# Second mixer: decay chain and gate rows in PSUM, weight splits between the activations, gate products at the third tile

## The reference

```
z = a_lr @ w_alpha_up + b_alpha
log_a = log_sigmoid(z) / 16                       # 4 heads x 128 channels
G = cumsum(log_a) within a chunk
q_dec = q * 128**-0.5 * exp(G); k_inv = k * exp(-G)
A = causal(q_dec @ k_inv.T); o = A @ v + (state carried from the chunks before)
sv = layer_norm(gelu(sv), ln_w, ln_b)             # the two gate rows ln_w, ln_b
s = causal(sgu_w) @ sv + sgu_b                    # 8 groups, chunks of 128 positions
merged = sigmoid(g_a) * rms(o) * silu(r) + sigmoid(g_b) * gelu(su) * s
```

## Time and profile before

| | |
|---|---|
| time, median of 3 runs | 1384.27 us (1382.73 to 1386.12) |
| profiled execution, first to last instruction | 1383.7 us; no other time of that execution is listed |
| PE busy | 98% of the span |
| POOL, DVE, ACT busy | 76%, 57%, 52% |
| granted TensorE clock, mean | 0.994 |

### The profile page before, as it was taken

One profiled execution on the slowest core, in us unless ns is written; L12 is line 12 of the kernel. 1 busy time (PEld: TensorE's weight loads), 2 busy tenths in 40 slices (PEclk: granted clock), 3 DMA queues, 4 the chain that ended last, 5 costly groups with the idle time before them and its releaser, 6 DMA issues.

```text
span 1383.7 us, 27404 instructions
## 1 busy us (share of the span) xinstructions
PE 1354.1 (98%) x9123; PEld 1178.4 (85%) x9123; DVE 788.2 (57%) x1616; ACT 713.0 (52%) x1139; POOL 1056.8 (76%) x466
## 2 busy tenths in 40 slices
PE   8999999999998999999999999999999999999997
PEld 8788999998776887899999988888788888888886
DVE  4755433336159327269990388888877878411113
ACT  7355655555364444435556544444455555566564
POOL 6655788886777786868888877777667777888885
PEclk9999999999999999999999999999999999999999
DMA  8444777774644456745555544454444445565552
GB/s 315 170 169 165 249 282 284 279 257 142 214 148 156 141 178 259 243 138 184 181 183 181 177 164 167 167 167 164 168 140 167 168 166 168 187 236 197 192 189 105
DMA packets 73057, 263.10 MB, mean 190 GB/s; under 512 B 8224, under 2 KB 9120, under 8 KB 72624
## 3 DMA queue, kind: packets, MB, share of 16 engines
q1 hardware_dynamic: 73008, 262.46, 55.0%
HBM read 259.81 MB, written 2.62 MB: 190 GB/s over the span
## 4 chain that ended last, share of the span: by engine, by line
PE 90%; DVE 5%; ACT 2%; issue 1%; DMA 1%; POOL 1%; SPq 0%; POOLq 0%; ACTq 0%; DVEq 0%
PE bank L964 14%; PE bank L965 14%; PE bank L966 14%; PE bank L945 10%; PE bank L922 8%; PE bank L924 8%; PE bank L923 8%; PE bank L946 5%; PE bank L1436 3%; PE bank L949 1%; DVE arena L1956 1%; PE bank L948 1%; PE bank L1108 1%; POOL wlo L448 1%; PE bank L1418 1%
## 5 line engine op out<-in xcount | busy, mean ns | idle before, releaser
L448 POOL TENSOR_TENSOR wlo<-raw,whi 128x1024 fp32r<-128x1024 f32 x432 | 1043.0, 2426 | 293.8 <-ACT whi L526 292.5
L526 ACT ACTIVATE whi<-raw 128x1024 fp32r<-128x1024 f32 x432 | 455.5, 1057 | 337.3 <-PE bank L966 254.2
L964 PE MATMUL bank<-whi,xhl 128*128 128x512 f32 x800 | 320.3, 400 | 12.7 <-DVE arena L1929 5.6
L966 PE MATMUL bank<-whi,xhl 128*128 128x512 f32 x800 | 313.9, 392 | 0.0
L965 PE MATMUL bank<-wlo,xhl 128*128 128x512 f32 x800 | 313.6, 392 | 0.0
L922 PE MATMUL bank<-xhl,whi 128*128 128x256 f32 x896 | 255.0, 285 | 1.9 <-DVE xhl L1516 1.1
L923 PE MATMUL bank<-xhl,whi 128*128 128x256 f32 x896 | 253.5, 283 | 0.0
L924 PE MATMUL bank<-xhl,wlo 128*128 128x256 f32 x896 | 253.4, 283 | 0.0
L945 PE MATMUL bank<-xhl,whi 128*128 128x512 f32 x616 | 222.0, 399 | 1.0 <-DVE xhl L1511 1.0
L964 PEld LDWEIGHTS bank<-whi,xhl 128*128 128x128 f32 x800 | 151.5, 189 | 48.7 <-issue 6.7
L966 PEld LDWEIGHTS bank<-whi,xhl 128*128 128x128 f32 x800 | 151.5, 189 | 32.8
(11 more groups left out here) (321 smaller groups left out, 1511.0 us busy)
## 6 DMA issues: line engine op xcount, KB each, us to landing
raw<-stream SPq DMA_DIRECT2D x432, 512.0 KB, 3.3
arena<-ada SPq DMA_DIRECT2D x48, 512.0 KB, 4.9
arena<-rows SPq DMA_DIRECT2D x5, 512.0 KB, 7.6
xs<-x SPq DMA_DIRECT2D x2, 512.0 KB, 6.5
arena<-rows SPq DMA_DIRECT2D x1, 1024.0 KB, 5.7
x_spill<-xs SPq DMA_DIRECT2D x1, 1024.0 KB, 6.3
xs<-x_spill SPq DMA_DIRECT2D x1, 1024.0 KB, 5.5
arena<-hgmask SPq DMA_DIRECT2D x1, 512.0 KB, 8.3
```

Of the source, the lines that this page charges most:

```text
L448: nc.gpsimd.tensor_tensor(wlo[:, slot, :], raw[:, slot, :], whi[:, slot, :].bitcast(F32), ALU.subtract).then_inc(lo_done, 1)
L526: nc.scalar.activation(whi[:, slot, :], raw[:, slot, :], ACT.Copy).then_inc(hi_done, 1)
L964: nc.tensor.matmul(bank[b][:, :], ah[:, ts], whi[:, slot, cs], start=start, stop=False)
L966: last = nc.tensor.matmul(bank[b][:, :], al[:, ts], whi[:, slot, cs], start=False, stop=final)
```

## The change

- **POOL**: the `lo` of su3 stands ahead of the variance root, not behind it.
- **ACT**: the two gate rows are copied from SBUF to PSUM, row 0 to banks 4 and 5 ahead of sv7's split, row 1 to banks 6 and 7 after su4's split. The splits of su3, su4 and of v1 to r2 are put one or two at a time between the activations. The logarithm and the exponentials are written to PSUM, in halves of two heads (128 x 512).
- **DVE**: the mask of the gating weights stands first, then the mean, then z and |z|. The layer norm runs in pieces of 512 columns with the gate rows from PSUM. Log-decays and running sums lie in banks 4 to 7; the sums at positions 63 and 127 of each chunk are copied to a small tile `g_at`. The products with q and k take the exponential from PSUM; those and the differences for the off-diagonal block stand ahead of the read-out of `m_v`, the last two products behind it.
- **PE**: the spatial gating products move from before r1 to before r2, and wait for all four steps of the q and k products (`g_qk`).

```diff
 POOL
             los(T_IN2_F + R - 1, T_IN2_M + 8 + R - 1)
+            lo((T_IN2_M + 11) % R, T_IN2_M + 12)
             root(S("squares"), squared("sgv"), s_(SS["sgv"]), rs("sgv"), 1.0 / D)
-            los(T_IN2_M + 8 + R - 1, T_IN2_M + 40 + R - 1)
+            los(T_IN2_M + 12, T_IN2_M + 40 + R - 1)
 ACT
+            his(T_IN2_F + R + 3, T_IN2_M + 7)
+            act.wait_ge(S("xg_out"), 4)
+            act.wait_ge(S("consts2_in"), 96)
+            for b in range(2):
+                nc.scalar.activation(bank[4 + b][:, :], rw[:, 0, b * 512:(b + 1) * 512], ACT.Copy)\
+                    .then_inc(S("rw_copied"), 1)
+            his(T_IN2_M + 7, T_IN2_M + 8 + 3)
             read_out("m_sv", T_IN2_M + 8, msv, ACT.Gelu, st[:, 2 * SS["sgs"]:2 * SS["sgs"] + 4])
+            upper_of(T_IN2_M + 11, T_IN2_M + 12)
...
+            upper_of(T_IN2_M + 12, T_IN2_M + 13)
+            act.wait_ge(S("z_out"), 1)
...
             read_out("m_su", T_IN2_M + 16, msu, ACT.Gelu)
+            upper_of(T_IN2_M + 19, T_IN2_M + 20)
             act.wait_ge(S("z_abs"), 1)
             own(nc.scalar.activation(t1, t1, ACT.Exp, scale=-1.0))
+            upper_of(T_IN2_M + 20, T_IN2_M + 21)
             own.sync()
+            act.wait_ge(S("sv_done"), 2)
+            for p in range(2):
+                nc.scalar.activation(heads(4 + p), t1[:, 2 * p:2 * p + 2, :], ACT.Ln, bias=1.0).then_inc(S("z_ln"), 1)
+            upper_of(T_IN2_M + 21, T_IN2_M + 24)
             act.wait_ge(S("g_diff"), 1)
+            for p in range(2):
+                nc.scalar.activation(heads(6 + p), t1[:, 2 * p:2 * p + 2, :], ACT.Exp, scale=1.0 / 16)\
+                    .then_inc(S("g_dec"), 1)
+            upper_of(T_IN2_M + 24, T_IN2_M + 25)
+            for p in range(2):
+                act.wait_ge(S("g_q"), p + 1)
+                nc.scalar.activation(heads(6 + p), t1[:, 2 * p:2 * p + 2, :], ACT.Exp, scale=-1.0 / 16)\
+                    .then_inc(S("g_dec"), 1)
+            upper_of(T_IN2_M + 25, T_IN2_M + 27)
             act.wait_ge(S("g_diffx"), 1)
...
 PE
-                if k != 1:
+                if k != 2:
                     return
                 pe.wait_ge(S("sgw_masked"), 1)
                 pe.wait_ge(S("sv_done"), 2)
+                pe.wait_ge(S("g_qk"), 4)
...
-            pe.wait_ge(S("g_qk"), 2)
 DVE
+            for p in range(2):
+                v.wait_ge(S("z_ln"), p + 1)
+                own(stt(heads(6 + p), t2[:, 2 * p:2 * p + 2, :], 0.0, heads(4 + p), ALU.min, ALU.subtract))
+            own.sync()
+            for p in range(2):
+                for j in range(2 * TT):
+                    ts = slice(j * P, (j + 1) * P)
+                    own(nc.vector.tensor_tensor_scan(bank[4 + p][:, ts], ones, bank[6 + p][:, ts], 0.0,
+                                                     ALU.mult, ALU.add))
+            own.sync()
+            for p in range(2):
+                own(nc.vector.tensor_copy(g_at[:, 4 * p:4 * p + 4, :], chunk_sums(p)[:, :, 63:P:64]))
+            own.sync()
+            for p in range(2):
+                last = ttt(t1[:, 2 * p:2 * p + 2, :].rearrange("p a (b c) -> p (a b) c", b=2), chunk_sums(p),
+                           g_at[:, 4 * p:4 * p + 4, 0:1].to_broadcast([P, 4, P]), ALU.subtract)
+            last.then_inc(S("g_diff"), 1)
...
             read_out("m_v", T_IN2_M + 24, mv, "v_out")
+            v.wait_ge(S("g_dec"), 5)
```

More of the change, by code:

```diff
@@ L270, in build @@
         gain = take(16)
+        g_at = take(16, 8, 2)
         top[0] = shared
@@ L788, in _ @@
                                      accum_out=s_(SS["sgv"])[:, tt:tt + 1]).then_inc(S("squares"), 1)
-            his(T_IN2_M + 8 + 3, T_IN2_M + 16 + 3)
+            upper_of(T_IN2_M + 12, T_IN2_M + 13)
+            act.wait_ge(S("z_out"), 1)
+            for b in range(2):
+                nc.scalar.activation(bank[6 + b][:, :], rw[:, 1, b * 512:(b + 1) * 512], ACT.Copy)\
+                    .then_inc(S("rw_copied"), 1)
+            his(T_IN2_M + 13, T_IN2_M + 17)
+            upper_of(T_IN2_M + 17, T_IN2_M + 19)
@@ L790, in _, with heads @@
             read_out("m_su", T_IN2_M + 16, msu, ACT.Gelu)
+            upper_of(T_IN2_M + 19, T_IN2_M + 20)
+            def heads(b):
+                return bank[b][:, :].rearrange("p (a t) -> p a t", a=2)
             act.wait_ge(S("z_abs"), 1)
             own(nc.scalar.activation(t1, t1, ACT.Exp, scale=-1.0))
+            upper_of(T_IN2_M + 20, T_IN2_M + 21)
             own.sync()
-            nc.scalar.activation(t1, t1, ACT.Ln, bias=1.0).then_inc(S("z_ln"), 1)
-            his(T_IN2_M + 16 + 3, T_IN2_M + 24 + 3)
+            act.wait_ge(S("sv_done"), 2)
@@ L801, in _ @@
-            nc.scalar.activation(t1[:, :, P:T], tG[:, :, P:T], ACT.Exp, scale=1.0 / 16).then_inc(S("g_dec"), 1)
+            for p in range(2):
[6 more added lines that the diff above has]
+                    .then_inc(S("g_dec"), 1)
@@ new lines, in _ @@
+            upper_of(T_IN2_M + 25, T_IN2_M + 27)
+            act.wait_ge(S("g_diffx"), 1)
+            nc.scalar.activation(bank[6][:, :].rearrange("p (a t) -> p a t", a=4), t1[:, :, 0:P], ACT.Exp,
+                                 scale=-1.0 / 16).then_inc(S("g_dec"), 1)
+            for p in range(2):
+                nc.scalar.activation(bank[7][:, p * T:(p + 1) * T].rearrange("p (a t) -> p a t", a=2),
+                                     heads(4 + p)[:, :, P:T], ACT.Exp, scale=1.0 / 16).then_inc(S("g_dec"), 1)
@@ L1924, in _ @@
             nc.vector.tensor_copy(alT, bank[6][0:16, 0:T]).then_inc(S("alr_out"), 1)
+            v.wait_ge(S("consts2_in"), 96)
+            ttt(sgw, sgw, caus.unsqueeze(1).to_broadcast([P, 8, P]), ALU.mult).then_inc(S("sgw_masked"), 1)
             def read_out(group, tiles_end, dst, done):
@@ L1930, in read_out @@
                         .then_inc(S(done), 1)
[L1933 to L1937, removed]
             v.wait_ge(S("sv_out"), 4)
@@ L1942, in _ @@
             tsc(s_(SS["sgm"]), s_(SS["sgm"]), -1.0 / D, None, ALU.mult).then_inc(S("sg_mean"), 1)
-            v.wait_ge(S("consts2_in"), 96)
-            ttt(sgw, sgw, caus.unsqueeze(1).to_broadcast([P, 8, P]), ALU.mult).then_inc(S("sgw_masked"), 1)
-            v.wait_ge(S("roots"), rooted("sgv"))
+            v.wait_ge(S("z_mm"), 1)
+            for h in range(4):
+                last = tsc(t2[:, h, :], bank[6 + h // 2][:, (h % 2) * T:(h % 2 + 1) * T], c_("balpha", h), None, ALU.add)
+            last.then_inc(S("z_out"), 1)
@@ L1946, in _ @@
+            v.wait_ge(S("z_out"), 1)
+            stt(t1, t2, -1.0, t2, ALU.mult, ALU.max).then_inc(S("z_abs"), 1)
             v.wait_ge(S("sg_mean"), 1)
             for tt in range(TT):
[L1948 to L1956, removed]
-            own.sync()
-            v8 = lambda t_: t_.rearrange("p a (b c) -> p (a b) c", b=2)
-            ttt(v8(t1), v8(tG), v8(tG)[:, :, 63:64].to_broadcast([P, 8, P]), ALU.subtract).then_inc(S("g_diff"), 1)
-            read_out("m_v", T_IN2_M + 24, mv, "v_out")
@@ L1962, in _ @@
[L1962 to L1969, removed]
+                v.wait_ge(S("squares"), squared("sgv", tt + 1))
@@ new lines, in _ @@
+                for b in range(2):
+                    cs = slice(b * 512, (b + 1) * 512)
+                    v.wait_ge(S("rw_copied"), b + 1)
+                    own(stt(msv[:, tt, cs], msv[:, tt, cs], s_(SS["sgm"])[:, tt:tt + 1], bank[4 + b][:, :],
+                            ALU.add, ALU.mult))
+            v.wait_ge(S("roots"), rooted("sgv"))
+            own.sync()
+            for tt in range(TT):
+                for b in range(2):
+                    cs = slice(b * 512, (b + 1) * 512)
+                    v.wait_ge(S("rw_copied"), b + 3)
+                    last = stt(msv[:, tt, cs], msv[:, tt, cs], rs("sgv", tt), bank[6 + b][:, :], ALU.mult, ALU.add)
+                last.then_inc(S("sv_done"), 1)
@@ new lines, in _, with chunk_sums @@
+            own.sync()
+            def chunk_sums(p):
+                return bank[4 + p][:, :].rearrange("p (a c) -> p a c", a=4)
+            for p in range(2):
+                own(nc.vector.tensor_copy(g_at[:, 4 * p:4 * p + 4, :], chunk_sums(p)[:, :, 63:P:64]))
+            own.sync()
+            for p in range(2):
+                last = ttt(t1[:, 2 * p:2 * p + 2, :].rearrange("p a (b c) -> p (a b) c", b=2), chunk_sums(p),
+                           g_at[:, 4 * p:4 * p + 4, 0:1].to_broadcast([P, 4, P]), ALU.subtract)
@@ new lines, in _ @@
+            last.then_inc(S("g_diff"), 1)
+            for p in range(2):
+                v.wait_ge(S("g_dec"), p + 1)
+                stt(t2[:, 2 * p:2 * p + 2, :], heads(6 + p), 128 ** -0.5, qk[:, 2 * p:2 * p + 2, :], ALU.mult, ALU.mult)\
+                    .then_inc(S("g_q"), 1)
+            for p in range(2):
+                v.wait_ge(S("g_dec"), p + 3)
+                ttt(t3[:, 2 * p:2 * p + 2, :], heads(6 + p), qk[:, 4 + 2 * p:6 + 2 * p, :], ALU.mult)\
+                    .then_inc(S("g_qk"), 1)
@@ new lines, in _ @@
```

(11 more changed lines are left out.)

4 lines of the change are left out of this document (removed).

## The result

The changed kernel takes 1372.62 us (median of four runs, 1371.22 to 1373.27), the kernel before, run beside it, 1383.72 (four runs, 1382.73 to 1386.12). The ratio is 0.9914, interval 0.9902 to 0.9927, so the change gains 10.1 to 13.6 us. The forecast was 1370.9 with a range from 1368.5 to 1378.5: faster, as forecast, and 1.7 us above the single number. The profiled execution of after is the run of 1373.27; its span is 1371.1.

What follows compares the result with a forecast made beforehand. The prediction took PE, busy 98% of the span, to bound the kernel. Removing 13.38 us of waits and low clock from the profiled 1383.7 gave 1370.3; carrying 0.57 gave 1370.9 us, range 1368.5 to 1378.5.

Steps and rivals of the forecast that it cites:

- Bound and ceiling: Second mixer: PE bounds the kernel; its waits and low clock there cost 13.38 us, the most the change can give.
- The first copy of `m_v`: DVE's read-out of bank 0 before r0: complete at 427.3, copied by 427.9, needed by r0 at 429.3.
- the last products: DVE's two last products, which PE's gating products await: done at 431.4, PE comes at 434.7, 3.3 to spare.
- ga0: First tile of the ga group, after the second mixer's tiles: to start near 457.3 instead of 470.7.
- Sums: DVE's eight running sums of 128 columns, one operand in PSUM: 0.35 each, 2.8 for eight, instead of 2.47 apiece.
- layer norm: DVE's layer norm in eight pieces from PSUM at 0.69: about 5.5 instead of 13.6, done by 397.
- the later of the two times worked out for su4: POOL's remainder of su4: done by 392.7 to 393.8, the later if |z| takes turns with POOL; needed at 396.6.
- The slipped chain: Rival: the ACT and DVE chain is 4 us beyond its 2.6 slack at r0, giving 1377.6; chance 0.10.
- Turns with one operand in SBUF: Rival: one SBUF operand suffices for turns with POOL; three sums at 2.47, five at 0.35, +6.2; 1378, chance 0.05.
- A slow sum by itself: Rival: each running sum costs 2.47 with or without POOL, PE idles 14.4 at r0; 1388, chance 0.04.
- Given back later: Rival: PE's waits behind the ga and gb groups end at a fixed time, so nothing is gained; 1384.3, chance 0.05.
- 1384.27, 0.57 above; I carry that: Last term of the sum: the runs' median 1384.27 is 0.57 above the profiled 1383.7, added to 1370.3.

Runs made afterwards that it cites:

- e1: Kernel before with only the new order at the head of su (remainder and split of su3 moved ahead); 1382.07 us, ratio 0.9991.
- e3: Kernel before with both the new order at the head of su and the running sums reading PSUM; 1375.01 us, ratio 0.9934.
- e7: Changed kernel with the eight running sums computed twice; 1371.45 us, ratio 0.9907 to the kernel before.
- e8: Changed kernel with the eight running sums computed four times; 1377.07 us, ratio 0.9947 to the kernel before.
- e10: Changed kernel with eleven more running sums within SBUF, on data nothing reads again, behind the gating products; 1370.18 us (one run).
- e9: Changed kernel with the variance root again ahead of su3's remainder and both splits behind the squares; 1370.29 us, ratio 0.9904 to the kernel before.
- e6: Changed kernel with the gating products again before the second tile, r1; 1372.50 us, ratio 0.9908 to the kernel before.
- e5: Changed kernel with the running sums' input back in SBUF; 1375.61 us, ratio 0.9925 to the kernel before.
- e4: Changed kernel with the splits of v5 to r2 in a row ahead of the exponentials; 1378.42 us, ratio 0.9966 to the kernel before.
- e2: Kernel before with only the log-decays written to PSUM, so the running sums read them there; 1375.60 us, ratio 0.9944.

## Why the prediction was right, and where its number was off

**Bound and ceiling: right.** 13.38 at most; 13.19 came, the whole stretch at the clean pace.

**Step by step.** After ran 1.72 late at su0 (387.35 against 385.63), so its times less 1.72 are compared. The first copy of `m_v` starts at 427.45 (worked out: 427.3); the last products end at 431.38 (431.4); ga0 starts at 457.26 (457.3). Sums 0.33 (0.35); layer norm 5.43 (5.5); operations with one operand in PSUM 0.68 (0.69). |z| did have to take its turn, 2.53 for 1.23, and POOL's root lasted 1.05 + 0.70; the later of the two times worked out for su4 covered this, and PE did not notice.

**What each part is worth,** in the order in which the runs add them: sums from PSUM 8.31 (84.82 to 76.51), layer norm from PSUM 2.45 more (to 74.06), order and the rest 2.43 (to 71.63). So PSUM carries 10.8 of 13.2, and the order and the rest 2.4. The 8.31 holds the idle time before r0 and the low clock behind it. These are the shares of this sequence; another one moves them (order first: 2.59, then the sums 7.29, by e1 and e3).

**Rivals.** The slipped chain didn't come: there is no wait at r0, and e7 and e8 show 4.0 of slack. Turns with one operand in SBUF: no, sums at 0.33 beside POOL's 2.38 (its delay was added up 0.16 short: three sums at 2.47 and five at 0.35 are 6.36 more than 2.8, not 6.2). A slow sum by itself: no (e10). Given back later: the time from ga0 to the end is 912.12 against 913.25, so nothing was.

**The term of the sum that was off is the last one,** "1384.27, 0.57 above; I carry that". I took the distance between a span and a median for the time outside the span. All four runs of after have 2.2 to 2.3 between span and time (1373.27 and 1371.1 in the profiled one). With 2.2 in place of 0.57 the sum is 1372.5; the forecast span was 1370.3, the four measured ones are 1368.9 to 1371.1. The error behind it: a profiled execution of before with a span of 1383.7 is not a median one. In seven runs of before beside e10, the distance was 1.8 to 1.9, and a median of 1383.69 has a span of 1381.9.

That the forecast span lies among the measured ones is in part luck. Starting from the median would have given 1370.9 again, and after would still be 1.7 above. The medians gained 11.10 where the stretch gained 13.19, and 2.09 are missing. Some 0.3 to 0.4 of them lie outside the span: 2.2 to 2.3 in every run of after, 1.8 to 1.9 in the runs of before that are on record with a span. (It isn't the change as such: e7, e8 and e10 have 1.8 to 1.9 too. What sets it is open.) For the rest, the profiled executions show two places outside the stretch where the clock falls in some executions and not in others.

The first is ahead of the change. The window at 326 to 332 of after is shown above, at clock 0.50; the same window of e9 has

```profile
326.00:332.00 6.00, 6.00 (x44) 5.07 (x44) 4.89 (x14) 4.56 (x12) 1.64 (x4) 1.00 0.20 76
```

with 44 products done for 25. The same run of small products, from the first one of 128x1 at L1173 to the first at L1180 (other lines in the others), takes 10.45 in after (322.30 to 332.75) and 7.40 in before and in e9. After began it 1.22 ahead of before, and so comes 1.8 late out of it and 1.72 late to su0. The second place is behind ga0, where PE waits 2.6 for DVE in each of these executions. The 8 us that follow, in before, after and e9:

```profile
999.15:1007.15 8.00, 7.88 (x22) 6.29 (x23) 5.43 (x11) 3.02 (x7) 2.55 (x2) 0.61 0.34 125
987.68:995.68 8.00, 7.79 (x45) 6.21 (x46) 5.52 (x11) 3.38 (x8) 3.42 (x2) 0.79 0.36 126
985.54:993.54 8.00, 7.46 (x53) 6.13 (x54) 6.66 (x14) 4.65 (x10) 4.72 (x3) 1.00 0.40 132
```

The time from ga0 to the end goes with it: 913.25, 912.12 and 910.8. Before's profiled execution was slowed most at the second place and not at the first; after's was slowed at both, at the first by some 3. The profiled executions with the same stretch fall into line: e9 and e10, quiet at both, took 1369.93 and 1370.18, e7 (0.72 at the first place) 1370.49, after (0.50) 1373.27 and e6 (0.57) 1374.03. The code up to the first place is the same in all of these, and e3 and e5 had the dip too, so it isn't put down to the change. That dips make up what is missing in the medians as well is likely, not shown, since the other executions have no trace. What decides in which executions the clock falls is open; no run aimed at it.

## What to carry to other kernels

When two engines look slow side by side, look for one operation that has two prices in the same trace; a cheap price beside the busy neighbour shows which operand to move, and here one operand gave 8.3 us. Then ask of every step in the chain whether it is late or merely queued: two reorderings cost nothing when undone (e6, e9), and one, of the splits, cost 7.4 (e4), because another reordering had made it necessary. Make the sum against a span with what lies outside it measured, and check that the profiled execution is a typical one, before arguing over the last two microseconds.

## What the runs showed of the hardware

**The turns cost a short instruction most.** A sum of 128 columns with both operands in SBUF goes from 0.33 to 2.45 beside a remainder, while the remainder goes from 2.39 to 2.46 at most (e10): the short instruction pays nearly everything. POOL pays too beside long passes: its remainders took 2.85 beside the layer norm, and its root 1.05 in after, beside |z|, for 0.19 in before. With one operand in PSUM neither pays (0.33 and 2.38 in after). The Trainium skill, SBUF — State Buffer, section "Who interferes with whom", states the rule as two SBUF inputs of DVE against a reading GpSimd, with at most one SBUF input free of it; e2, e5 and e10 agree.

**A source in PSUM costs no more here.** 512 columns took 0.68 to 0.69 from PSUM in after, 692 ns from SBUF in the earlier trace rows. The Trainium skill's VectorE: DVE Perf Modes, section on the TRN2 errata, gives a PSUM source 120 fixed cycles and an SBUF source 58. The 65 ns between them, an estimate from that page, didn't show.

**Idle time of PE can have a second price, and its size varies.** Waits of 0.3 to 0.9 (e2) left the granted clock at 1.00. Behind 2.50 of idle it was 0.64 over the next 3.30 (e5), behind 3.94 it was 0.55 over 3.76 (e8), behind 4.44 it was 0.50 over 5.56 (e4), as behind the 5.75 of the earlier trace rows. But behind the same 5.75 it was back at 1.00 after some 4 in e1, and behind one and the same wait of 2.6, after ga0, it was 0.61, 0.79 or 1.00 over 8 us. And the clock can dip with no wait before it, between small products, as at 326 to 332.
